# The up projection's 576 token columns cut at 384 in place of 288

## The chip, the cores and the metric

The kernel runs on one NeuronCore of one Trainium2 chip. The metric is device time in microseconds (us) of one execution; a lower number is better. Three timed runs of the kernel before took 1313.4, 1313.48 and 1315.09 us, a median of 1313.48 us. The profile is that of a further execution, whose span from the first to the last instruction was 1312.0 us. Instruction durations are in nanoseconds (ns).

## The reference, cut to what matters

The program is one layer of a hybrid decoder for 512 prompt tokens and 8 sequences of 8 sample tokens, 576 token columns in all. After a recurrent branch, an attention branch and their merge comes the part that the change touches, the gated feed-forward block with a short convolution over time:

```python
h2 = rmsnorm(x, norm2_g)
up, new_conv_f = causal_dwconv(jnp.einsum('btd,df->btf', h2, w_up), ffn_conv0, conv_f_w, conv_f_b)
gf, vf = jnp.split(up, 2, axis=-1)
x = x + jnp.einsum('btf,fd->btd', jax.nn.gelu(gf) * vf, w_down)
```

Here x has 1024 features, `w_up` is 1024 x 6144 and `w_down` 3072 x 1024, all float32. `causal_dwconv` adds three shifted copies of the rows, each scaled per feature, with two rows of state in front of every sequence.

## The kernel before, in words

Everything is kept with features on the 128 partitions and the 576 tokens along the free dimension: columns 0 to 511 are the prompt, 512 to 575 the eight samples.

A projection is made of **units**. One unit gives 128 output features for all 576 tokens and is accumulated in one of the two-bank PSUM tensors `ps[0]` and `ps[1]`, by turns (`ps[u % 2]`). Its first 288 token columns lie at element 0 (the first bank), the other 288 at element 512 (the second). `HALF` is 288. A unit of eight row tiles (k = 0 to 7) has 48 matmuls. To keep precision, weights and activations are each split into a rounded part and the rest (`w_hi`, `w_lo`, `h_hi`, `h_lo`, of type float32r), and three of the four products are added: `w_hi` by `x_hi`, `w_hi` by `x_lo`, `w_lo` by `x_hi`. Each product is two matmuls, one for each half of the tokens, with the same 128 x 128 weights. In the instruction stream each of these matmuls has a weight load (LDWEIGHTS) of its own ahead of it. All of this is `looped_unit` (L490 to L506), which `unit` (L486) calls, and which the other projections use too.

The feed-forward block has 24 **pairs** of up units, one for the gate features and one for the value features, so 48 up units, in three rounds, each followed by 8 down units. The order of work on TensorE is written out by hand: L833 to L835 are the first pair, `pairs` (L822) holds a loop over the other 8, 8 and 7 of a round, and `down` (L829) a down unit. A unit waits for its weights (`lo_ready`) and for its PSUM tensor to be free (`acc_free`).

Weights come by DMA on SyncE's queue, up to four units ahead (L348). ScalarE rounds them to `w_hi` (L862) and VectorE takes the difference to `w_lo` (L1168), each two units ahead of use.

When an up unit is done, VectorE runs `ffn_conv` (L1465): three multiplications by the reciprocal norm `rinv2` read the unit's columns from PSUM and put them in `ug` or `uv`: L1474 takes columns 0 to 287, L1475 columns 288 to 511, and L1476 the 64 sample columns, which go to a layout with room for the state rows. The third frees the PSUM tensor. Then come the difference of the next weights, three instructions of the convolution, and, after the pair's second unit, the product of gate and value (L1492 to L1505).

Of the kernel before, what the change touches and what calls it, by code (L numbers as in the profile page):

```python
# [7 lines left out]
ALU = mybir.AluOpType  # L8
# [6 lines left out]
KT = D // P  # L15
SEQ = 512
NB, NT = 8, 8
NS = NB * NT
TOK = SEQ + NS
HALF = TOK // 2  # L20
PAST = 256
NG, NH, HD = 3, 4, 128
AW = NG * NH * HD
# [25 lines left out]
UPAD, USEQ = 2, 2 + NT  # L49
US0 = UPAD + SEQ  # L50
UW = US0 + NB * USEQ
# [24 lines left out]
def up_unit(i):  # L76

    return U_FFN + 2 * i + KT * min((i - 1) // PPR if i else 0, NRND - 1)


def down_unit(r, m):
    pairs = min((r + 1) * PPR + 1, NPAIR)
    return U_FFN + 2 * pairs + KT * r + m
# [24 lines left out]
def build(nc, t):  # L108
# [33 lines left out]
    nkt = [u.shape[1] for u in units]  # L142

    ctx = ExitStack()
    with ctx:
        def sb(name, shape, dt=F32, at=ctx):
            return at.enter_context(nc.sbuf_tensor(name, shape, dt))
# [14 lines left out]
        h_hi = sb("h_hi", [P, KT, TOK], F32R)  # L162
        with ExitStack() as m:
            x_t = sb("x_t", [P, KT, TOK], at=m)
        h_lo = sb("h_lo", [P, KT, TOK], F32R)
# [74 lines left out]
        rinv2 = sb("rinv2", [P, TOK])  # L240
# [20 lines left out]
        ps = [ctx.enter_context(nc.psum_tensor(f"ps{i}", [P, 1024], F32)) for i in range(4)]  # L261
        acc = [p[:, :].rearrange("p (h n) -> p h n", h=2)[:, :, 0:HALF] for p in ps]
        NORM, TRN = 2, 3
# [37 lines left out]
        def diag(row):  # L301

            return row.rearrange("p (b n) -> p b n", n=NS + NT)[:, :, 0:NT]
# [32 lines left out]
        def seqs(ap, width):  # L336
            return ap.rearrange("p (b n) -> p b n", n=width)
# [145 lines left out]
        def _(pe):  # L483
            mm, tr = pe.matmul, pe.transpose

            def unit(u, x_hi, x_lo, ready=None, between={}):  # L486

                looped_unit(u % 2, nkt[u], u + 1, u // 2, x_hi, x_lo, ready, between)

            def looped_unit(p, n, parts, freed, x_hi, x_lo, ready=None, between={}):  # L490


                pe.wait_ge(lo_ready, parts)
                if not (isinstance(freed, int) and freed == 0):
                    pe.wait_ge(acc_free[p], freed)
                for k in range(n):
                    if k in between:
                        between[k]()
                    if ready:
                        ready(k)  # L500
                    for w, x in ((w_hi, x_hi), (w_hi, x_lo), (w_lo, x_hi)):
                        for h in range(2):
                            last = mm(ps[p][:, 512 * h:512 * h + HALF], w[:, p, k, :],  # L503
                                      x[:, k, HALF * h:HALF * (h + 1)],
                                      start=(k == 0 and x is x_hi and w is w_hi), stop=(k == n - 1 and w is w_lo))
                last.then_inc(unit_done, 1)  # L506

            def feature_sum(src, k, n):

                for h in range(2):  # L510
                    last = mm(ps[NORM][:, 512 * h:512 * h + HALF], ones, src[:, HALF * h:HALF * (h + 1)],  # L511
                              start=(k == 0), stop=(k == n - 1))
# [7 lines left out]
            for c in range(KT):  # L520
                last = tr(ps[NORM][:, c * NS:(c + 1) * NS], x_tok[0:NS, 4, c * P:(c + 1) * P], ident[0:NS, 0:NS])
# [240 lines left out]
            for c in range(KT):  # L762
                last = tr(ps[2][0:36, c * P:(c + 1) * P], l_st[:, c, :], ident)
            last.then_inc(lst_ps, 1)

            with pe.Fori(0, KT - 2) as i:
                for j, (tiles, hi, lo) in enumerate(((KT, h_hi, h_lo), (NH, att_hi, att_lo), (KT, h_hi, h_lo), (KT, y_hi, y_lo))):
                    u = U_MRG + 5 + j
                    looped_unit(u % 2, tiles, i * 4 + (u + 1), i * 2 + u // 2, hi, lo)
# [5 lines left out]
            def x2_products(c):  # L775

                if c < KT:
                    if c == 0:
                        pe.wait_ge(x2_in, 32)
                    else:  # L780
                        pe.wait_ge(x2_cp, c)
                    for n in range(4):
                        tr(ps[3][:, n * P:(n + 1) * P], x_tok2[:, n, c * P:(c + 1) * P], ident)
                    tr(ps[3][:, SEQ:TOK], x_tok2[0:NS, 4, c * P:(c + 1) * P], ident[0:NS, 0:NS]).then_inc(x2_ps, 1)
                if c:
                    pe.wait_ge(ones_rdy, 1)
                    pe.wait_ge(sq2_hi_rdy, c)
                    pe.wait_ge(sq2_lo_rdy, c)
                    for part in (sq2_hi, sq2_lo):
                        for h in range(2):  # L790
                            last = mm(ps[NORM][:, 512 * h:512 * h + HALF], ones_r[:, :],  # L791
                                      part[:, (c - 1) % 2, HALF * h:HALF * (h + 1)],
                                      start=(c == 1 and part is sq2_hi), stop=(c == KT and part is sq2_lo))
                    last.then_inc(sq2_used, 1)
# [27 lines left out]
            def pairs(first, count):  # L822

                with pe.Fori(0, count) as i:
                    for j in range(2):
                        u = up_unit(first) + j
                        looped_unit(u % 2, KT, i * 2 + (u + 1), i + u // 2, h_hi, h_lo)

            def down(r, m):  # L829
                unit(down_unit(r, m), g_hi[r % 2], g_lo[r % 2],  # L830
                     (lambda k: (pe.wait_ge(g_hi_rdy, r * PPR + k + 1), pe.wait_ge(g_lo_rdy, r * PPR + k + 1))) if m == 0 else None)

            unit(up_unit(0), h_hi, h_lo, lambda k: (pe.wait_ge(xg2_hi, k + 1), pe.wait_ge(xg2_lo, k + 1)),  # L833
                 {KT - 3: lambda: x2_products(KT)})
            unit(up_unit(0) + 1, h_hi, h_lo)  # L835
            for r in range(NRND):
                pairs(r * PPR + 1, min(PPR, NPAIR - 1 - r * PPR))
                down(r, 0)
# [1 line left out]
                if r < NRND - 1:  # L840
                    down(r, 1)
                    with pe.Fori(0, KT // 2 - 1) as i:
                        for j in range(2):
                            u = down_unit(r, 2) + j
# [316 lines left out]
        def _(dve):  # L1161
            STT, TT, TS = dve.scalar_tensor_tensor, dve.tensor_tensor, dve.tensor_scalar

            def lo_split(u):
                if u >= U_ALL:
                    return
                dve.wait_ge(hi_ready, u + 1)
                TT(w_lo[:, u % NSPL, 0:nkt[u], :], w_raw[:, u % NRAW, 0:nkt[u], :],  # L1168
                   w_hi[:, u % NSPL, 0:nkt[u], :], ALU.subtract).then_inc(lo_ready, 1)
# [128 lines left out]
            for hp in range(NH):  # L1298
# [18 lines left out]
                for g in range(NG):  # L1317
                    last = dve.tensor_copy(diag(q_dia[:, g, :]), qT[:, g, SEQ:TOK].rearrange("p (b t) -> p b t", b=NB))
                last.then_inc(q_dia_rdy, 1)
                for b in range(0, NB, 2):  # L1320
                    n = hp * NB + b
# [93 lines left out]
            for n, (kind, m) in enumerate(MERGE):  # L1415
                u = U_MRG + n
# [23 lines left out]
            for c in range(KT):  # L1440
                u = U_OUT + c
# [18 lines left out]
            def flinked(ins):  # L1460
                ins.then_inc(f_link, 1)
                flink[0] += 1
                dve.wait_ge(f_link, flink[0])

            def ffn_conv(i, j):  # L1465
                u, ti = up_unit(i) + j, i + j * FT
                x, y, v = (uv if j else ug)[:, i % 2, :], cv if j else cg, ft[:, ti, :]
                flinked(dve.tensor_copy(seqs(x[:, US0:UW], USEQ)[:, :, 0:UPAD], seqs(v[:, F_S:F_N], 2)))

                dve.wait_ge(unit_done, u + 1)  # L1470
                if i >= 2:
                    dve.wait_ge(fst_rdy, i - 1)
                p_ = ps[u % 2]
                TT(x[:, UPAD:UPAD + HALF], p_[:, 0:HALF], rinv2[:, 0:HALF], ALU.mult)  # L1474
                TT(x[:, UPAD + HALF:US0], p_[:, 512:512 + SEQ - HALF], rinv2[:, HALF:SEQ], ALU.mult)  # L1475
                TT(seqs(x[:, US0:UW], USEQ)[:, :, UPAD:USEQ], seqs(p_[:, 512 + SEQ - HALF:512 + HALF], NT),  # L1476
                   seqs(rinv2[:, SEQ:TOK], NT), ALU.mult).then_inc(acc_free[u % 2], 1)
                lo_split(u + NSPL)
                dve.wait_ge(acc_free[u % 2], u // 2 + 1)
                if j == 0 and i:  # L1480
                    dve.wait_ge(gm_rdy, i)
                flinked(TS(y[:, :], x[:, 0:CW], v[:, F_W:F_W + 1], v[:, F_B:F_B + 1], ALU.mult, ALU.add))
                flinked(STT(y[:, :], x[:, 1:1 + CW], v[:, F_W + 1:F_W + 2], y[:, :], ALU.mult, ALU.add))
                STT(y[:, :], x[:, 2:2 + CW], v[:, F_W + 2:F_W + 3], y[:, :], ALU.mult, ALU.add).then_inc(cv_rdy if j else cg_rdy, 1)
# [22 lines left out]
            for kind, i, m in ffn_steps():  # L1507
# [4 lines left out]
                else:  # L1512
                    u = down_unit(i, m)
# [6 lines left out]
def constants(np):  # L1520
# [13 lines left out]
    t = t[:, None]  # L1534
    k = np.arange(PAST)[None, :]
    own = [np.arange(P)[None, :] >= t,
# [34 lines left out]
```

## Time and profile before

| | |
|---|---|
| Median of the timed runs | 1313.48 us (1313.4 to 1315.09) |
| The profiled execution: span (the page gives no time beside it) | 1312.0 us |
| TensorE matmuls | busy 1269.2 us, 97% of the span, 9313 instructions |
| TensorE weight loads | busy 1223.8 us, 93%, 9313 instructions |
| VectorE | busy 727.9 us, 55% |
| ScalarE | busy 487.1 us, 37% |
| GpSimd | busy 167.0 us, 13% |

A matmul's record lasts from its start to the modelled end of its last column's way through the array, so records of matmuls that follow each other overlap. How fast they go is read from the distance between their starts, or from the time of a row that merges many, divided by their number. A row "x2" that starts at 786.07 and lasts 0.30 us, of instructions of 0.19 us each, has starts 0.30 - 0.19 = 0.11 us apart. The same goes for weight loads, which stand under PEld.

### The profile page before, as it was taken

What the parts mean: (1) busy time and instruction counts of PE and PEld (TensorE: products, weight loads), DVE (VectorE), ACT (ScalarE), POOL (GpSimd) and SP (SyncE); (2) the same over time, 40 slices, a digit from 0 to 9 for tenths busy, and PEclk for the clock granted to TensorE, in tenths of its full rate; (3) what the DMA queues carried; (4) which work ended last, traced back from release to release, by engine and by line L of the source; (5) the groups of instructions that cost most, each with busy time, mean ns of one, the idle gap of its engine ahead of it and who ended that gap; (6) DMA issues with size and microseconds to landing.
All of it is one profiled execution on the core that took longest, in us unless ns stands there. A gap on an engine that the chain in (4) does not pass through costs nothing.

```text
span 1312.0 us, 22213 instructions
## 1 busy us (share of the span) xinstructions
PE 1269.2 (97%) x9313; PEld 1223.8 (93%) x9313; DVE 727.9 (55%) x1212; ACT 487.1 (37%) x713; POOL 167.0 (13%) x255
## 2 busy tenths in 40 slices
PE   7899999999999999998999999999999999999996
PEld 6898998998899789998999999999999999999996
DVE  4973383283374348883333344788735886368821
ACT  4444444343443348774222234422222223122231
POOL 1271601601601100001000000000010001000021
PEclk9899999999999999999999999999999999999998
DMA  7382532522523112225323222232222223222321
GB/s 207 64 209 59 145 93 77 146 77 70 148 74 95 42 49 67 79 57 141 88 81 88 79 73 78 77 87 80 80 85 80 80 80 85 80 85 84 88 64 45
DMA packets 180436, 117.13 MB, mean 89 GB/s; under 512 B 6844, under 2 KB 172890, under 8 KB 180345
## 3 DMA queue, kind: packets, MB, share of 16 engines
q1 hardware_dynamic: 168944, 87.34, 23.5%
q0 software_dynamic: 11392, 28.79, 8.0%
q8 instruction: 49, 0.80, 0.3%
q14 instruction: 23, 0.19, 0.1%
q10 hardware_dynamic: 28, 0.01, 0.0%
HBM read 107.66 MB, written 8.45 MB: 89 GB/s over the span
## 4 chain that ended last, share of the span: by engine, by line
PE 92%; DVE 3%; ACT 2%; issue 1%; DMA 1%; POOL 0%; SPq 0%; ACTq 0%; POOLq 0%; DVEq 0%
PE ps L503 76%; PE ps L666 4%; PE ps L511 2%; PE ps L625 2%; PE ps L735 1%; PE ps L611 1%; PE ps L600 1%; DMA x_tok<-in_x_prompt 1%; PE ps L643 1%; PE ps L588 1%; DVE prob L1268 1%; DVE hn L1201 1%; ACT w_hi L862 0%; PE ps L791 0%; PE ps L808 0%
## 5 line engine op out<-in xcount | busy, mean ns | idle before, releaser
L503 PE MATMUL ps<-h_hi,w_hi 128*128 128x288 f32 x1824 | 404.0, 303 | 7.5 <-DVE h_lo L1204 3.9
L503 PE MATMUL ps<-h_hi,w_lo 128*128 128x288 f32 x1824 | 392.5, 297 | 0.0
L503 PE MATMUL ps<-h_lo,w_hi 128*128 128x288 f32 x1824 | 391.9, 297 | 0.0
L1168 DVE TENSOR_TENSOR w_lo<-w_raw,w_hi 128x1024 fp32r<-128x1024 f32 (+1 forms) x164 | 196.0, 1195 | 282.3 <-ACT w_hi L862 282.2
L862 ACT ACTIVATE w_hi<-w_raw 128x1024 fp32r<-128x1024 f32 (+1 forms) x164 | 170.3, 1038 | 445.3 <-PE ps L503 438.3
L503 PEld LDWEIGHTS ps<-h_hi,w_hi 128*128 128x128 f32 x1824 | 296.5, 190 | 12.4 <-issue 4.3
L503 PEld LDWEIGHTS ps<-h_lo,w_hi 128*128 128x128 f32 x1824 | 295.4, 190 | 0.0
L503 PEld LDWEIGHTS ps<-h_hi,w_lo 128*128 128x128 f32 x1824 | 295.3, 190 | 0.0
L1243 DVE RECIPROCAL qk_ri<-qk_rt 128x576 f32<-128x576 f32 x24 | 90.0, 3750 | 26.6 <-ACT qk_rt L941 26.6
L467 POOL DMA_DIRECT2D out<-f_row x12 | 6.2, 515 | 624.7 <-ACT f_row L1139 624.7
L503 PE MATMUL ps<-g_hi,w_hi 128*128 128x288 f32 x384 | 83.0, 297 | 1.6 <-DVE g_lo L1505 1.6
L503 PE MATMUL ps<-g_lo,w_hi 128*128 128x288 f32 x384 | 82.0, 295 | 0.0
L503 PE MATMUL ps<-g_hi,w_lo 128*128 128x288 f32 x384 | 82.0, 295 | 0.0
L503 PEld LDWEIGHTS ps<-g_hi,w_hi 128*128 128x128 f32 x384 | 61.5, 188 | 1.9 <-ACT g_hi L1132 1.8
L503 PEld LDWEIGHTS ps<-g_lo,w_hi 128*128 128x128 f32 x384 | 61.8, 188 | 0.0
L503 PEld LDWEIGHTS ps<-g_hi,w_lo 128*128 128x128 f32 x384 | 61.7, 188 | 0.0
L1132 ACT ACTIVATE g_hi<-gm 128x576 fp32r<-128x576 f32 x24 | 16.5, 686 | 91.8 <-DVE gm L1494 91.8
L625 PE MATMUL ps<-kcT,q_dia 128*64 128x128 f32 (+1 forms) x192 | 33.8, 315 | 1.4 <-DVE kcT L1325 1.4
L1325 DVE COPY kcT<-ps 128x512 f32<-128x512 f32 x16 | 11.1, 691 | 41.9 <-PE ps L611 41.9
L625 PEld LDWEIGHTS ps<-kcT,q_dia 128*64 128x64 f32 x192 | 22.0, 136 | 11.4 <-issue 4.0
L1268 DVE CUSTOM_DVE_ANT_0 prob<-ps,masks 128x512 f32<-128x512 f32 (+3 forms) x40 | 20.4, 546 | 18.9 <-PE ps L602 18.9
L1285 DVE TENSOR_SCALAR o_sb<-ps,stat 128x128 f32<-128x128 f32 (+1 forms) x20 | 7.0, 349 | 41.5 <-issue 32.0
(281 smaller groups left out, 1781.6 us busy)
## 6 DMA issues: line engine op xcount, KB each, us to landing
w_raw<-in_w_in SPq DMA_DIRECT2D x68, 512.0 KB, 3.9
w_raw<-in_w_up SPq DMA_DIRECT2D x48, 512.0 KB, 3.9
w_raw<-in_w_down SPq DMA_DIRECT2D x24, 512.0 KB, 3.9
vc<-in_cache_v_g POOLq DMA_DIRECT2D x12, 512.0 KB, 6.2
kc<-in_cache_k_g POOLq DMA_DIRECT2D x48, 128.0 KB, 3.1
w_raw<-in_w_br_a SPq DMA_DIRECT2D x8, 512.0 KB, 3.9
w_raw<-in_w_out SPq DMA_DIRECT2D x8, 512.0 KB, 3.9
x_tok<-in_x_prompt SPq DMA_DIRECT2D x4, 512.0 KB, 9.7
```

The lines of the kernel that those rows point to most:

```text
L503: last = mm(ps[p][:, 512 * h:512 * h + HALF], w[:, p, k, :], x[:, k, HALF * h:HALF * (h + 1)], start=(k == 0 and x is x_hi and w is w_hi), ...
L511: last = mm(ps[NORM][:, 512 * h:512 * h + HALF], ones, src[:, HALF * h:HALF * (h + 1)], start=(k == 0), stop=(k == n - 1))
L588: tr(bank[:, r * P:(r + 1) * P], src[:, r * P:(r + 1) * P], ident)
L600: mm(s[:, 0:SEQ], qT[:, 0, rows], kT[:, 0, 0:SEQ], start=True, stop=True)
L611: last = tr(bank[:, i * P:(i + 1) * P], kc[:, n % NKC, i, :], ident)
L625: last = mm(ps[2][0:NS, c0:c0 + cn], q_dia[:, g, (b - 1) * NS:b * NS], kcT[:, n % 2, c0:c0 + cn], start=(b == 1 and g == 0), stop=(b == NB ...
L666: last = mm(o_bank(hp, i), p_, v_, start=(n == 0), stop=(n == len(srcs) - 1))
L862: A(w_hi[:, u % NSPL, 0:nkt[u], :], w_raw[:, u % NRAW, 0:nkt[u], :], ACT.Copy).then_inc(hi_ready, 1)
L1132: A(g_hi[r % 2][:, i % PPR, :], gm[:, :], ACT.Copy).then_inc(g_hi_rdy, 1)
L1168: TT(w_lo[:, u % NSPL, 0:nkt[u], :], w_raw[:, u % NRAW, 0:nkt[u], :], w_hi[:, u % NSPL, 0:nkt[u], :], ALU.subtract).then_inc(lo_ready, 1)
L1243: dve.reciprocal(qk_ri[:, :], qk_rt[:, :]).then_inc(qk_rinv, 1)
L1268: last = dve.tensor_tensor_reduce(prob[0:rows, e % 2, s0:s0 + n], sc[0:rows, s0:s0 + n], masks[0:rows, m - C_PM:m - C_PM + n], SCALE, -3e3 ...
```

## The change

In the 48 up units, and only there, the first piece of the token columns becomes 384 wide (columns 0 to 383, at element 0 of the PSUM tensor) and the second 192 (columns 384 to 575, at element 512). `looped_unit` takes the width of the first piece as an argument, 288 unless told otherwise. The number of matmuls and weight loads, the total of the columns, the weights and the PSUM tensors are the same. In `ffn_conv` the reads follow: L1474 takes 384 columns, L1475 128, and L1476 the same 64 sample columns from their new place in the second bank.

```diff
+WIDE = 384
@@ looped_unit
-                        for h in range(2):
-                            last = mm(ps[p][:, 512 * h:512 * h + HALF], w[:, p, k, :],
-                                      x[:, k, HALF * h:HALF * (h + 1)],
+                        for at, c0, c1 in ((0, 0, first), (512, first, TOK)):
+                            last = mm(ps[p][:, at:at + c1 - c0], w[:, p, k, :], x[:, k, c0:c1],
                                       start=(k == 0 and x is x_hi and w is w_hi), stop=(k == n - 1 and w is w_lo))
@@ pairs, and the same at the two units of the first pair
-                        looped_unit(u % 2, KT, i * 2 + (u + 1), i + u // 2, h_hi, h_lo)
+                        looped_unit(u % 2, KT, i * 2 + (u + 1), i + u // 2, h_hi, h_lo, first=WIDE)
@@ ffn_conv
-                TT(x[:, UPAD:UPAD + HALF], p_[:, 0:HALF], rinv2[:, 0:HALF], ALU.mult)
-                TT(x[:, UPAD + HALF:US0], p_[:, 512:512 + SEQ - HALF], rinv2[:, HALF:SEQ], ALU.mult)
-                TT(seqs(x[:, US0:UW], USEQ)[:, :, UPAD:USEQ], seqs(p_[:, 512 + SEQ - HALF:512 + HALF], NT),
+                TT(x[:, UPAD:UPAD + WIDE], p_[:, 0:WIDE], rinv2[:, 0:WIDE], ALU.mult)
+                TT(x[:, UPAD + WIDE:US0], p_[:, 512:512 + SEQ - WIDE], rinv2[:, WIDE:SEQ], ALU.mult)
+                TT(seqs(x[:, US0:UW], USEQ)[:, :, UPAD:USEQ], seqs(p_[:, 512 + SEQ - WIDE:512 + TOK - WIDE], NT),
```

TensorE's order at the passage from the output projection (`mg_hi`, `mg_lo`: the merged branches) to the first up unit (`h_hi`, `h_lo`), before:

```order
L503 MATMUL ps<-mg_hi,w_hi 128x288 x2
L503 MATMUL ps<-mg_lo,w_hi 128x288 x2
L503 MATMUL ps<-mg_hi,w_lo 128x288 x2
L503 MATMUL ps<-h_hi,w_hi 128x288 x2
L503 MATMUL ps<-h_lo,w_hi 128x288 x2
L503 MATMUL ps<-h_hi,w_lo 128x288 x2
```

The same engine in the body of the loop over pairs, after the change, which has put the matmul on line 504:

```order
L504 MATMUL ps<-h_hi,w_hi 128x384
L504 MATMUL ps<-h_hi,w_hi 128x192
L504 MATMUL ps<-h_lo,w_hi 128x384
L504 MATMUL ps<-h_lo,w_hi 128x192
L504 MATMUL ps<-h_hi,w_lo 128x384
L504 MATMUL ps<-h_hi,w_lo 128x192
```

Nothing changes places; each couple of equal matmuls has become a wide one and a narrow one. VectorE's order at a gate unit, before and then after (`ft` holds the convolution's weights, `ps` the PSUM tensor):

```order
L1468 COPY ug<-ft 128x8x2
L1474 TENSOR_TENSOR ug<-ps,rinv 128x288
L1475 TENSOR_TENSOR ug<-ps,rinv 128x224
L1476 TENSOR_TENSOR ug<-ps,rinv 128x8x8
L1168 TENSOR_TENSOR w_lo<-w_raw,w_hi 128x1024
```

```order
L1468 COPY ug<-ft 128x8x2
L1474 TENSOR_TENSOR ug<-ps,rinv 128x384
L1475 TENSOR_TENSOR ug<-ps,rinv 128x128
L1476 TENSOR_TENSOR ug<-ps,rinv 128x8x8
L1168 TENSOR_TENSOR w_lo<-w_raw,w_hi 128x1024
```

Only the widths of the first two reads differ.

## Rows read from the trace of the kernel before

**Rows 1.** The profile page: span, engines, and granted clock in 40 slices

```profile
span 1312.0 us, 22213 instructions
PE 1269.2 (97%) x9313; PEld 1223.8 (93%) x9313; DVE 727.9 (55%) x1212; ACT 487.1 (37%) x713; POOL 167.0 (13%) x255
...
PEclk9899999999999999999999999999999999999998
```

**Rows 2.** Windows over the three rounds of up units: busy time of each engine

```profile
core 0: us, PE busy (x) PEld busy (x) DVE busy (x) ACT busy (x) POOL busy (x), PEclk, DMA share, GB/s
826.00:942.00 116.00, 116.00 (x872) 115.95 (x871) 95.86 (x200) 34.56 (x40) 0.00 (x0) 1.00 0.29 85
...
996.00:1098.00 102.00, 102.00 (x767) 102.00 (x766) 80.01 (x172) 25.90 (x30) 0.00 (x0) 1.00 0.29 82
...
1151.00:1240.00 89.00, 89.00 (x670) 89.00 (x669) 69.51 (x149) 22.41 (x26) 0.00 (x0) 1.00 0.29 83
```

**Rows 3.** Chain that ended last, from 826 us: start us, us, what, number

```profile
831.81 117.57 PE ps L503 x882
949.38 1.75 PE ps L808 x16
951.13 153.52 PE ps L503 x1152
1104.65 1.75 PE ps L808 x16
1106.39 134.03 PE ps L503 x1008
1240.50 1.07 ACT w_hi L862
```

**Rows 4.** Timeline of weight loads at 900 us, in an up unit

```profile
start us, us, engine line op out<-in xcount [idle before <-releaser]
...
900.02 0.32 PEld L503 LDWEIGHTS ps<-h_hi,w_lo 128*128 128x128 f32 x2
900.29 0.33 PEld L503 LDWEIGHTS ps<-h_hi,w_hi 128*128 128x128 f32 x2
```

**Rows 5.** Timeline of matmuls at 900 us, in an up unit

```profile
900.15 0.43 PE L503 MATMUL ps<-h_hi,w_lo 128*128 128x288 f32 x2
900.42 0.42 PE L503 MATMUL ps<-h_hi,w_hi 128*128 128x288 f32 x2
```

**Rows 6.** Groups of weight loads by form: busy us, mean ns of one

```profile
L503 PEld LDWEIGHTS ps<-h_hi,w_hi 128*128 128x128 f32 x1824 | 296.5, 190 | 12.4 <-issue 4.3 <-DVE w_lo L1168 3.3 <-ACT h_hi L895 1.3
...
L666 PEld LDWEIGHTS ps<-vc,p_dia 128*64 128x64 f32 x256 | 27.8, 137 | 0.5
L666 PEld LDWEIGHTS ps<-v_tok,probT 128*128 128x128 f32 x192 | 22.9, 192 | 0.0
```

**Rows 7.** Timeline of weight loads after an idle stretch at 785.9 us

```profile
785.86 0.14 PEld L784 LDWEIGHTS ps<-const,x_tok 64*128 64x128 f32 x1 [0.17 <-issue]
786.07 0.30 PEld L791 LDWEIGHTS ps<-sq_hi,ones_r 128*128 128x128 f32 x2
```

**Rows 8.** Timeline of weight loads at 133 us, in the attention

```profile
132.97 0.30 PEld L602 LDWEIGHTS ps<-kT,qT 128*128 128x128 f32 x2
133.19 0.75 PEld L666 LDWEIGHTS ps<-v_tok,probT 128*128 128x128 f32 x6
```

**Rows 9.** Timeline of matmuls at 132 us, in the attention

```profile
132.00 1.02 PE L600 MATMUL ps<-kT,qT 128*128 128x512 f32 x2
132.86 0.38 PE L601 MATMUL ps<-kT,qT 128*128 128x128 f32 x2
```

**Rows 10.** Timeline of matmuls at 18.7 us, plain float32 of 288 columns

```profile
18.75 1.14 PE L511 MATMUL ps<-sq,const 128*128 128x288 f32 x4
```

**Rows 11.** Groups of matmuls by form: busy us, mean ns of one

```profile
L511 PE MATMUL ps<-qk_sq,const 128*128 128x288 f32 x96 | 27.6, 411 | 0.0
```

**Rows 12.** Groups of VectorE by form, 826 to 942 us

```profile
L1474 DVE TENSOR_TENSOR ug<-ps,rinv 128x288 f32<-128x288 f32 x9 | 4.1, 458 | 0.3
...
L1475 DVE TENSOR_TENSOR ug<-ps,rinv 128x224 f32<-128x224 f32 x9 | 3.4, 380 | 0.0
```

More of the change, by code:

```diff
@@ L484, in _, with unit, looped_unit @@
             mm, tr = pe.matmul, pe.transpose
-            def unit(u, x_hi, x_lo, ready=None, between={}):
-                looped_unit(u % 2, nkt[u], u + 1, u // 2, x_hi, x_lo, ready, between)
-            def looped_unit(p, n, parts, freed, x_hi, x_lo, ready=None, between={}):
+            def unit(u, x_hi, x_lo, ready=None, between={}, first=HALF):
+                looped_unit(u % 2, nkt[u], u + 1, u // 2, x_hi, x_lo, ready, between, first)
+            def looped_unit(p, n, parts, freed, x_hi, x_lo, ready=None, between={}, first=HALF):
                 pe.wait_ge(lo_ready, parts)
@@ L833, in _ @@
             unit(up_unit(0), h_hi, h_lo, lambda k: (pe.wait_ge(xg2_hi, k + 1), pe.wait_ge(xg2_lo, k + 1)),
-                 {KT - 3: lambda: x2_products(KT)})
-            unit(up_unit(0) + 1, h_hi, h_lo)
+                 {KT - 3: lambda: x2_products(KT)}, first=WIDE)
+            unit(up_unit(0) + 1, h_hi, h_lo, first=WIDE)
             for r in range(NRND):
```

## The prediction, made before the changed kernel was run

> **What bounds the kernel now.** I read the page first: its engine rows show TensorE busy for 97% of the span, and the clock row full speed nearly throughout [rows 1]. The windows over the rounds of up units then show that nothing but TensorE counts there: it is busy for all of 116.00, 102.00 and 89.00 us, at a granted clock of 1.00 (the 2.4 GHz level), while VectorE has 95.86, 80.01 and 69.51 us and ScalarE less [rows 2]. The chain of waits says the same: three unbroken runs of L503 matmuls [rows 3]. So each nanosecond that an up unit gains or loses on TensorE is one of the total.
>
> Next, the pace inside such a run. 117.57 us for 882 matmuls is 133.3 ns from one to the next, 153.52 us for 1152 is 133.3, 134.03 us for 1008 is 133.0 [rows 3]. I take 133.3 ns, and 266.6 ns for a couple (the two pieces of one product). 288 columns at one per cycle of 2.4 GHz are 120.0 ns, so 13.3 ns of each interval is something else.
>
> Last, the weight loads, since each matmul has one. A load starts with the matmul ahead of it: loads at 900.02 and 900.29, matmuls at 900.15 and 900.42, each row a couple some 0.13 us apart, so that the second load of the row at 900.02 goes out with the matmul at 900.15 [rows 4, 5]. The load is hidden under a running matmul, and under one only. How long must that matmul be?
>
> - A load of 64 columns lasts 137 ns, one of 128 columns 192 [rows 6]: 55 ns for 64 columns, so 110 ns for the stream of 128 and the rest a fixed way through. The loads of L503 have the same form and 190 ns [rows 6].
> - After an idle stretch, when no earlier matmul holds anything up, two float32r loads start 0.30 - 0.19 = 0.11 us apart [rows 7]. The second can only be waiting for the first to have streamed.
> - Six loads in a row in the attention start (0.75 - 0.19) / 5 = 0.112 us apart [rows 8]. Their matmuls of 128 plain float32 columns stream at two cycles a column, 107 ns, so this is at or just above the load's own time.
>
> So a load needs about 110 ns. Under a matmul of 288 columns it fits. 192 columns stream in 192 / 2.4 = 80 ns, and it doesn't.
>
> The Trainium skill says of this, in "TensorE: Matmul & The Clock Gate", section "LDWEIGHTS (loading the stationary operand)", that a load takes its columns divided by 1.2 GHz, which is 107 ns here. [...]
>
> **The change part by part.** 48 up units of 8 row tiles of 3 products are 1152 couples, which now take 1152 x 266.6 ns = 307.1 us.
>
> *The wide piece*, 384 columns. No row shows a float32r matmul of another width than 288. If the 13.3 ns is a fixed cost, the interval is 160.0 + 13.3 = 173.3 ns. If it grows with the columns, it is 133.3 x 384 / 288 = 177.7. Plain float32 matmuls stream at two cycles a column. Two of 512 columns take from 132.00 to 132.86 us [rows 9], 430 ns each, where the columns need 427; four of 288 start (1.14 - 0.41) / 3 = 0.243 us apart, where the columns need 240 [rows 10, 11]. There the cost on top is 3 ns at both widths. That speaks for a fixed one, and gives the lower bound: if the long matmul sheds what it doesn't share with the plain ones, 160 + 3 = 163 ns. I take 174, nearest to the fixed cost.
>
> *The narrow piece*, 192 columns. Streaming alone gives 133.3 - 96 / 2.4 = 93.3 ns, the lower bound, if the next load were hidden all the same. With the load as the limit it is 108 to 112 ns by rows 7 and 8. Should the 288-column stream's surplus over a plain one, some 10 ns, come on top, 122, the upper bound. I take 113, which is row 8's value and a nanosecond for the turn.
>
> *The sum of a couple* is 174 + 113 = 287 ns, 20.4 ns more than now. 1152 x 20.4 ns = 23.5 us.
>
> *VectorE's reads.* 288 columns take 458 ns and 224 take 380 [rows 12]: 1.22 ns a column. 384 and 128 columns come to 575 + 263 = 838 ns, as now. They lie beside TensorE, which is the slower by 20 us in the first round [rows 2], and if that cover were gone the difference would still be nothing. No wait, DMA or buffer is added, and a unit's PSUM tensor is freed by the same third read, a whole unit of 6.4 us before TensorE wants it. The engines that wait for TensorE wait 24 x 20.4 ns = 0.49 us a unit longer and hold up nobody.
>
> The profiled execution has 1312.0 us from first to last instruction; the median of the runs is 1313.48, that is 1.5 us around the span. 1312.0 + 23.5 + 1.5 = 1337.0 us.
>
> **The rivals.**
>
> *A. The load limits the narrow matmul* (the forecast). For it: rows 6 to 8, three readings of 108 to 112 ns. Its own range: from 163 + 108 = 271 ns a couple (+4.4, times 1152 = 5.1 us, 1319 us) to 177.7 + 122 = 299.7 (+33.1, 38.1 us, 1352 us). Most of it lies above 1328, since the fixed cost is better borne out than its loss.
>
> *B. Not slower: loads are taken further ahead.* TensorE might start a second load while a wide matmul still runs, so that the load for the piece after the narrow one is partly done in the 174 ns of the wide one. Over a couple there are 266 ns of matmul for 220 ns of loading, so from full freedom in the order on, nothing would be lost: a couple stays at 266.6 ns and the kernel at 1313.5 us. It decides if a load can start before the matmul ahead of it does. Against it: in rows 4 and 5 each load waits for the start of a matmul, although it could have gone out 20 ns earlier. It might go so far as a gain, if besides the wide piece sheds its surplus: 163 + 93.3 = 256.3 ns, 1152 x 10.3 ns = 11.9 us less, 1302 us. The Trainium skill, in "TensorE: Matmul & The Clock Gate", section "Step-by-step: what each phase is for", lets TensorE pull loads ahead of running matmuls into a background set of weights. If that set is one deep, rows 4 and 5 agree with it and it gives no help here.
>
> *C. A narrow float32r matmul goes at the plain float32 rate.* A float32r column now costs one cycle. A plain product has two records (the two matmuls of a norm sum stand as x4), each at two cycles a column [rows 10]. If the one-cycle rate did not hold for short matmuls, 192 columns would take 2 x (160 + 3) = 326 ns, a couple 174 + 326 = 500 ns, and the kernel 1152 x 233.4 ns = 268.9 us more, 1582 us. No row speaks for it or against it, since all float32r matmuls here have 288 columns; that the same instruction is issued in both cases speaks against.
>
> *D. The change doesn't do what it says*: the pieces could come out as before. The order of instructions shows 384 and 192 in all up units, so I give this nothing.
>
> **How the numbers follow.** A has 0.79, B without a gain 0.10, B with a gain 0.04, C 0.07. The time predicted is A's, 1337.0 us. The range reaches from A's low end, 1319, to 1350, just under its high one, and holds nearly all of A. A change within 0.2% of 1313.5 us (2.6 us) is what a measurement can't tell from none. Faster by more than that is B with a gain, 0.04; the same is B without, 0.10; slower is A and C, 0.86.
>
> **What would show it.** In the profile after, matmuls of L504 with 192 columns should be followed by the next start after 110 to 115 ns, those with 384 after 173 to 178, and 48 matmuls of an up unit should take 6.9 us where 6.4 stood. The loads under a wide matmul should start with it, as now, and the load that goes out with a narrow one should be followed at once by its matmul, 110 ns later. TensorE stays 100% busy in the rounds at clock 1.00. The down units, still of 288 columns, should keep 133.3 ns. I am wrong if the next matmul starts 93 ns after a narrow one (B), or 300 ns and more (C), or if the whole time moves by something that isn't 1152 times the change of a couple.

## The result and the profile after

The changed kernel takes 1334.19 us, the median of three runs (1333.94 to 1336.15), against 1313.48 us: a ratio of 1.0159 with a 95% interval from 1.0142 to 1.0175. That is 20.7 us slower; 1337.0 was forecast, in a range from 1319 to 1350.

The page of the kernel after has the same number of instructions as [rows 1], and the growth of the span is all TensorE's:

```profile
span 1332.2 us, 22213 instructions
PE 1289.6 (97%) x9313; PEld 1244.4 (93%) x9313; DVE 728.8 (55%) x1212; ACT 487.0 (37%) x713; POOL 167.0 (13%) x255
```

TensorE is busy for 20.4 us more, the span is 20.2 us longer, the other engines do what they did. The windows over the first two rounds of up units, which stand beside [rows 2], show TensorE, and beside its weight loads nothing else, busy all the time, at the same clock (the 2.4 GHz level):

```profile
826.00:950.00 124.00, 124.00 (x875) 124.00 (x874) 96.17 (x200) 34.61 (x40) 0.00 (x0) 1.00 0.28 80
1004.00:1116.00 112.00, 112.00 (x792) 112.00 (x791) 83.38 (x178) 26.91 (x32) 0.00 (x0) 1.00 0.26 75
```

The chain of waits has the same pieces as [rows 3] (start us, us, what, number):

```profile
831.78 124.99 PE ps L504 x882
956.77 1.75 PE ps L808 x16
958.52 160.35 PE ps L504 x1152
1118.87 1.75 PE ps L808 x16
1120.62 139.99 PE ps L504 x1008
...
1270.59 6.40 PE ps L504 x48
```

The three long runs are 7.42, 6.83 and 5.96 us longer, 20.2 us together, which is the whole growth of the span. The last row is a down unit, still at 6.40 / 48 = 0.133 us a matmul. The first run holds one such unit and 834 matmuls of up units, so these take (124.99 - 6.40) / 834 = 142.2 ns each, and a couple of wide and narrow **284.4 ns**. The same sum on [rows 3] gives (117.57 - 6.40) / 834 = 133.3 and 266.6. The difference, 17.8 ns, times 1152 is 20.5 us. I use this sum below for each experiment, from its own first run.

Inside a couple, first the weight loads and then the matmuls of the kernel after, as in [rows 4, 5]:

```profile
899.88 0.19 PEld L504 LDWEIGHTS ps<-h_hi,w_hi 128*128 128x128 f32 x1
900.06 0.30 PEld L504 LDWEIGHTS ps<-h_lo,w_hi 128*128 128x128 f32 x2
900.35 0.30 PEld L504 LDWEIGHTS ps<-h_hi,w_lo 128*128 128x128 f32 x2
```

```profile
899.77 0.25 PE L504 MATMUL ps<-h_hi,w_lo 128*128 128x192 f32 x1
899.86 0.45 PE L504 MATMUL ps<-h_hi,w_hi 128*128 128x384 f32 x2
900.15 0.45 PE L504 MATMUL ps<-h_lo,w_hi 128*128 128x384 f32 x2
900.43 0.45 PE L504 MATMUL ps<-h_hi,w_lo 128*128 128x384 f32 x2
```

The load at 900.06 goes out with a narrow matmul. The second load of its row starts 0.30 - 0.19 = 0.11 us later, at 900.17. But the wide matmul started at 900.15: for the first time a load goes out behind its matmul and not with it. It had to wait for the load before it. That load is through by 900.28 (0.11 us on), and yet the next one, at 900.35, waits for the narrow matmul, which starts then. The wide matmul's record begins 0.09 us after the narrow one's (899.77, 899.86), before its weights are all in, and the next start comes 0.20 us later (900.06).

The trace keeps starts in whole nanoseconds, and I take their means over the up units from 845 to 935 us. The next matmul starts 87.2 ns after a narrow one and 197.3 ns after a wide one. The load that goes out with a narrow matmul is followed by the next after 108.2 ns, and that one by the next after 176.3 ns. Both pairs add up to the couple. The kernel with a short load, below, shows that a wide matmul without a wait takes 176 ns; so the wait of 108.2 - 87.2 = 21 ns is booked inside the wide matmul.

### The profile page after: what moved, and what is told of

It is laid out like the page before. It is cut to its first block, busy times and chain, and to the rows that moved or that the text cites. A ratio compares the mean times of both kernels' runs of the same rounds, so it can differ in the third digit from the quotient of the medians.

```text
span 1332.2 us, 22213 instructions
## 1 busy us (share of the span) xinstructions
PE 1289.6 (97%) x9313; PEld 1244.4 (93%) x9313; DVE 728.8 (55%) x1212; ACT 487.0 (37%) x713; POOL 167.0 (13%) x255
## 4 chain that ended last, share of the span: by engine, by line
PE 92%; DVE 3%; ACT 2%; issue 1%; DMA 1%; POOL 0%; SPq 0%; ACTq 0%; POOLq 0%; DVEq 0%
PE ps L504 76%; PE ps L666 4%; PE ps L511 2%; PE ps L625 2%; PE ps L735 1%; PE ps L611 1%; PE ps L600 1%; DMA x_tok<-in_x_prompt 1%; PE ps L643 1%; PE ps L588 1%; DVE prob L1268 1%; DVE hn L1201 1%; ACT w_hi L862 0%; PE ps L791 0%; PE ps L808 0%
## 5 line engine op out<-in xcount | busy, mean ns | idle before, releaser
L504 PE MATMUL ps<-h_hi,w_hi 128*128 128x288 f32 (+2 forms) x1824 | 412.1, 307 | 7.4 <-DVE h_lo L1204 3.9
L504 PE MATMUL ps<-h_hi,w_lo 128*128 128x288 f32 (+2 forms) x1824 | 400.7, 302 | 0.0
L504 PE MATMUL ps<-h_lo,w_hi 128*128 128x288 f32 (+2 forms) x1824 | 399.0, 300 | 0.0
L504 PEld LDWEIGHTS ps<-h_hi,w_hi 128*128 128x128 f32 x1824 | 288.3, 191 | 12.3 <-issue 4.2
L504 PEld LDWEIGHTS ps<-h_lo,w_hi 128*128 128x128 f32 x1824 | 286.8, 190 | 0.0
L504 PEld LDWEIGHTS ps<-h_hi,w_lo 128*128 128x128 f32 x1824 | 286.8, 190 | 0.0
L1243 DVE RECIPROCAL qk_ri<-qk_rt 128x576 f32<-128x576 f32 x24 | 90.0, 3751 | 26.6 <-ACT qk_rt L941 26.6
L1132 ACT ACTIVATE g_hi<-gm 128x576 fp32r<-128x576 f32 x24 | 16.4, 685 | 91.3 <-DVE gm L1494 91.3
L1474 DVE TENSOR_TENSOR uv<-ps,rinv 128x384 f32<-128x384 f32 x24 | 13.4, 558 | 49.8 <-issue 47.6
L1268 DVE CUSTOM_DVE_ANT_0 prob<-ps,masks 128x512 f32<-128x512 f32 (+3 forms) x40 | 20.4, 546 | 18.8 <-PE ps L602 18.8
```

The lines of the kernel that those rows point to most:

```text
L504: last = mm(ps[p][:, at:at + c1 - c0], w[:, p, k, :], x[:, k, c0:c1], start=(k == 0 and x is x_hi and w is w_hi), stop=(k == n - 1 and w i ...
L1132: A(g_hi[r % 2][:, i % PPR, :], gm[:, :], ACT.Copy).then_inc(g_hi_rdy, 1)
L1243: dve.reciprocal(qk_ri[:, :], qk_rt[:, :]).then_inc(qk_rinv, 1)
L1268: last = dve.tensor_tensor_reduce(prob[0:rows, e % 2, s0:s0 + n], sc[0:rows, s0:s0 + n], masks[0:rows, m - C_PM:m - C_PM + n], SCALE, -3e3 ...
L1474: TT(x[:, UPAD:UPAD + WIDE], p_[:, 0:WIDE], rinv2[:, 0:WIDE], ALU.mult)
```

## The experiments

**Other widths.** One constant is changed, on the changed kernel:

```diff
-WIDE = 384
+WIDE = 320        # and 352, and 448
```

320 and 256 columns:

> Pieces of 320 and 256 columns in the up units, nothing else. Three theories for the 17.9 ns that a couple of 384 and 192 lost (284.5 ns against 266.6 in the rounds of up units). Load: a weight load takes 111 ns and goes out no sooner than the narrow matmul, so a couple takes 111.2 + 13.3 + (columns of the wide piece) / 2.4 ns, or 266.6 if that is more. Here 257.8, so 266.6 stands: 1313.5 us, no change. Wide: a matmul above 288 columns pays by itself, 20.7 us for 96 columns more, so 6.9 us for 32: 1320.4. Short: every matmul under 256 columns pays a fixed surplus; here there is none: 1313.5.

352 and 224:

> Pieces of 352 and 224 columns. Load: 111.2 + 13.3 + 146.7 = 271.2 ns a couple, 4.6 over 266.6, times 1152 = 5.3 us: 1318.8 us. Wide: 64 / 96 of 20.7 = 13.8 us: 1327.3. Short: the full surplus, 20.7 us: 1334.2.

448 and 128:

> Pieces of 448 and 128 columns. Load: 111.2 + 13.3 + 186.7 = 311.2 ns a couple, 44.6 over 266.6, 51.4 us: 1364.9 us. Wide: 160 / 96 of 20.7 = 34.5 us: 1348. Short: 20.7 us as for 192: 1334.2.

The kernel before, run beside these, had a median of 1312.65 us. 320/256 took 1314.38 us, a ratio of 1.0013 (0.9998 to 1.0027); 352/224 took 1320.39, 1.0058 (1.0037 to 1.0078); 448/128 took 1367.19, 1.0412 (1.0385 to 1.044). The first run of the chain of each:

```profile
832.43 117.59 PE ps L504 x882
```

```profile
831.82 120.35 PE ps L504 x882
```

```profile
833.15 137.05 PE ps L504 x882
```

By the sum above that is 266.6, 273.3 and 313.3 ns a couple, where the load theory had 266.6, 271.2 and 311.2. The first is that of the kernel before to the nanosecond, although its wide piece has 32 columns more, so the wide theory falls. The theory of a fixed fine for short matmuls falls with the other two: 224 columns lose 6.7 ns, 192 lose 17.8, 128 lose 46.7. The loads of 448/128 show why it is that many:

```profile
900.25 0.30 PEld L504 LDWEIGHTS ps<-h_hi,w_lo 128*128 128x128 f32 x2
900.56 0.30 PEld L504 LDWEIGHTS ps<-h_hi,w_hi 128*128 128x128 f32 x2
```

Under a narrow matmul of 53 ns of columns the two loads are again 0.30 - 0.19 = 0.11 us apart. In the kernel of 352 and 224 columns, with 93 ns, they are too:

```profile
900.15 0.30 PEld L504 LDWEIGHTS ps<-h_hi,w_lo 128*128 128x128 f32 x2
```

The load does not shrink with the matmul above it: in the means over 845 to 935 us the two are 108.3, 108.2 and 108.3 ns apart under 224, 192 and 128 columns. The rest of the couple, from the second load to the next couple's first, is 165.0, 176.3 and 205.0 ns for the wide pieces of 352, 384 and 448. The load theory had 111.2 for the load, a number that was set to fit the changed kernel's couple, and 160.0, 173.3 and 200.0 for the rest. The first is too long by 3 ns and the rest too short by 3 to 5, which leaves 2.1 ns of error at 352 and at 448.

**The narrow piece first.** `WIDE = 192`:

> Pieces of 192 and then 384 columns: the narrow matmul comes first in each couple. Load: each narrow matmul still has one load under it and there are as many of them, so 20.7 us as with 384 and 192: 1334.2 us; in the records the interval after the narrow one is again some 87 ns and that after the wide one 197. If instead the order mattered (the last matmul of a product, which is followed by other weights, being the narrow one), most of the 20.7 us would go: near 1314.

1339.13 us, a ratio of 1.0206 (1.018 to 1.0232) to the same 1312.65 us, and 290.0 ns a couple, from this row:

```profile
831.92 127.32 PE ps L504 x882
```

The loss is there, as the load theory had it, and is not removed by the order. But it is 5.6 ns a couple larger than with 384 first, which no theory had. The loads are again 108 ns apart under the narrow piece (means as above); it is the other distance that has grown, from 176 to 182 ns.

**A shorter load.** In up units alone the weights get 64 columns, so half of the up projection's output features are left out, with pieces of 288 and 288, and of 384 and 192:

```diff
-                            last = mm(ps[p][:, at:at + c1 - c0], w[:, p, k, :], x[:, k, c0:c1],
+                            last = mm(ps[p][0:feat, at:at + c1 - c0], w[:, p, k, 0:feat], x[:, k, c0:c1],
```

288 and 288:

> Up units with weights of 64 columns in place of 128 (the other 64 output features of each up unit are not computed), pieces of 288 and 288 as before. A load then has half the stream, some 55 ns. Load theory: nothing was limited by loads at 288, so the couple stays near 266.6 ns and the time near 1313.5 us. If the 13.3 ns that a 288-column interval has over its columns came from the load running beside it, the couple would fall towards 246 ns and the kernel by up to 1152 x 20.6 ns = 24 us. This is the base for the next kernel.

384 and 192:

> The same 64-column weights (half of the output features of the up units left out) with pieces of 384 and 192. Load: a load of some 55 ns fits under the narrow matmul of 80 ns, so the couple costs what it costs with 288 and 288 and the same weights: no difference from the kernel beside it, and the interval records go to some 93 and 173 ns. Wide or short theory: the loss is in the matmuls themselves, and this kernel is 20.7 us slower than the one beside it.

The two took 1310.03 and 1311.13 us, beside 1313.37 us of the kernel before. Their first runs of the chain, in this order:

```profile
830.98 116.21 PE ps L505 x882
```

```profile
831.82 116.49 PE ps L505 x882
```

That is 263.3 and 264.0 ns a couple. With a load of half the stream, 384 and 192 cost 0.7 ns a couple more than 288 and 288, where they cost 17.8 with the full load. The loads go out with their matmuls again, in the second of the two kernels:

```profile
900.21 0.22 PEld L505 LDWEIGHTS ps<-h_hi,w_lo 128*64 128x64 f32 x2
900.47 0.22 PEld L505 LDWEIGHTS ps<-h_hi,w_hi 128*64 128x64 f32 x2
```

Its groups have 134 ns for one of them (busy us, mean ns, idle before):

```profile
L505 PEld LDWEIGHTS ps<-h_hi,w_lo 128*64 128x64 f32 x768 | 85.5, 134 | 15.8
```

So the two of a row start 0.22 - 0.134 = 0.086 us apart, which is the narrow matmul's own interval (in the means of the matmuls' starts 87.6 ns, and 176.4 for a wide one), and the load engine now sits idle between them. This is the experiment that settles the cause: the matmuls stream as many columns as in the changed kernel, and the load is half as long. Each matmul also gives 64 outputs in place of 128, which can't be told apart from the load by this pair alone; but both together are worth only 3.3 ns to the couple of 288 and 288, and 20.4 ns (284.4 - 264.0) to that of 384 and 192. The even couple has 26.6 ns over its columns, and 23.3 of them stay with the load halved, so most of that surplus has another cause.

**More couples.** The changed kernel with the down units cut in the same way. The diff shows those in the loop; the others get `first=WIDE` too, and VectorE adds each down unit in two instructions in place of one:

```diff
-                            looped_unit(u % 2, PPR, i * 2 + (u + 1), i + u // 2, g_hi[r % 2], g_lo[r % 2])
+                            looped_unit(u % 2, PPR, i * 2 + (u + 1), i + u // 2, g_hi[r % 2], g_lo[r % 2], first=WIDE)
```

> The changed kernel with the 24 down units cut at 384 and 192 as well (VectorE then adds a down unit in two instructions of 384 and 192 columns in place of one). 576 more couples. Load: each loses the same 17.9 ns, 10.3 us on top of 1334.2: 1344.5 us, and the down units before the last round of them run 48 matmuls in 6.83 us in place of 6.40. If the loss belonged to the up units alone (their loop, or VectorE's reads), nothing would be added: 1334.2 us.

1344.89 us, 10.7 us over the changed kernel (the kernel before, beside this one and the next two, took 1313.62), and a down unit takes

```profile
1285.95 6.81 PE ps L504 x48
```

in place of 6.40. 576 more couples cost what half of 1152 did. So the loss isn't a matter of the up units, their loop or VectorE's reads of them.

**Order or place.** The two other combinations of which piece comes first in time and which columns it has. Both have this edit, and the second has `WIDE = 192` besides:

```diff
-                        for at, c0, c1 in ((0, 0, first), (512, first, TOK)):
+                        for at, c0, c1 in (((0, 0, first), (512, first, TOK)) if first == HALF else ((512, first, TOK), (0, 0, first))):
```

The change's places, narrow issued first:

> The change's pieces at the change's places (columns 0 to 383 at element 0, 384 to 575 at element 512), but in each couple the narrow matmul is issued first. It asks why the kernel with 192 columns first took 290.0 ns a couple (87.5 and 202.5) in place of 284.5. If the order in time is the reason (the wide matmul last in its product), 290 ns and 1152 x 5.5 ns = 6.3 us over the changed kernel, about 1340 us. If it was where the wide piece lies (columns 192 to 575, second bank), the couple is back at 284.5 ns and the time at 1334 us. The load theory alone gives 284.5 ns for either.

Columns 192 to 575 issued first, then 0 to 191:

> Columns 0 to 191 at element 0, 192 to 575 at element 512, and the wide matmul issued first. The fourth of the four combinations of order and place. Order as the reason for the 5.5 ns: 284.5 ns a couple, 1334 us. Place as the reason: 290 ns, 1340 us.

1338.63 and 1334.18 us. The first runs of the chain:

```profile
829.23 127.32 PE ps L504 x882
```

```profile
831.97 124.99 PE ps L504 x882
```

290.0 and 284.4 ns a couple. The narrow piece in front costs 5.6 ns a couple wherever its columns lie, so it is the order and not the place. What in the order does it isn't shown. With the narrow piece first, the matmul behind the wide one belongs to the next product, so it has other weights or the other part of the activations (`h_lo` for `h_hi`); a kernel that issues the same product twice would tell more, and was not run.

## Why the prediction was right

The mechanism of forecast A is borne out, step by step. Two sizes were off, in opposite directions, and so was the place where the wait would be seen.

- *TensorE sets the end and each nanosecond counts*: the runs of the chain grew by 20.2 us, the span by 20.2.
- *A load needs about 110 ns and only one matmul hides it*: 108 ns between loads under pieces of 224, 192 and 128 columns, with 93, 80 and 53 ns of columns. With the load halved 0.7 of the 17.8 ns are left. Rival B (loads further ahead) is out: the late load goes out once the one before has streamed, and the load after it waits for the next matmul's start, although the load engine is free 0.07 us before that (900.28, 900.35).
- *The sum of a couple*: 287 ns were forecast and 284.4 measured, so 23.5 us became 20.5. The narrow term was put at 113 ns and is 108.2, by the distance of the loads. It came from the attention's loads, 0.112 us apart, and a nanosecond for a turn; but the matmuls beside those loads themselves need 107 ns and some 3 on top, so that row was an upper bound. The wide term was put at 174 ns, with the fixed 13.3 on top of its columns, and is 176.3. The two errors, 4.8 too much and 2.3 too little, partly cancel, and that much of the nearness of 287 is luck.
- *Where the wait would be seen*: this part was wrong. I expected the next start 110 to 115 ns after a narrow matmul and 173 to 178 after a wide one. The rows have 0.09 and 0.20 us. The wide matmul's record begins before its weights are in, and the wait is in it. By my own test ("I am wrong if the next matmul starts 93 ns after a narrow one") the reading would have gone to rival B, and only the couple's sum and the delayed load tell the two apart. The test should have been on the distance of the loads. The 48 matmuls of an up unit, forecast at 6.9 us, take 24 x 284.4 ns = 6.83.
- *VectorE's reads*, forecast as 575 and 263 ns for the same 838 as before. The groups after have 558 and 281, 839 together:

```profile
L1474 DVE TENSOR_TENSOR ug<-ps,rinv 128x384 f32<-128x384 f32 x24 | 13.4, 558 | 8.2 <-issue 7.5
...
L1475 DVE TENSOR_TENSOR ug<-ps,rinv 128x128 f32<-128x128 f32 x24 | 6.7, 281 | 0.0
```

  The PSUM tensor was said to be free a whole unit of 6.4 us before TensorE wants it. In the trace of the kernel before, the third read of a gate unit ends at 899.87 us and the tensor is wanted at 904.4, so it is some 4.5 us. That is still ample.

- *Rival C*, a narrow float32r matmul at a quarter of the rate, is out: 128 columns beside 448 take 313.3 ns, where C's way of counting gives 2 x (128 x 2 / 2.4 + 3) = 219 ns for the narrow piece and at least 448 / 2.4 = 187 for the wide one, 406 together; and 0.7 ns is all that 192 columns lose once the load is short.
- *On top of the sum*: 1.5 us between span and median were assumed; it was 1334.19 - 1332.2 = 2.0.

## What to carry to other kernels

Where TensorE sets the time and every matmul reloads its weights, as here, each piece of moving columns has to be long enough to cover the next load by itself; what a longer neighbour has to spare helps nothing. The even cut is safe as long as its half covers a load; here 256 columns lose nothing and 224 already lose 6.7 ns a couple. Read that limit from the distance of two loads that nothing else holds up, and judge the result by the sum over a couple, not by the start of the next matmul.

## What the runs showed of the hardware

The time that a float32r matmul takes on top of its columns grows with their number here. With the load out of the way (64-column weights, 384 and 192), the next start comes 87.6 ns after the narrow matmul and 176.4 after the wide one: 7.6 and 16.4 ns over the columns, or 0.456 and 0.459 ns a column, where a cycle at the granted clock is 0.417. I had taken the 13.3 ns for a fixed cost, since plain float32 matmuls have 3 ns at either width [rows 9 to 11]. Pieces of 288 and 288 and of 320 and 256 come to the same 266.6 ns, which fits both readings, but the starts inside the second couple don't: 149.3 ns after 320 columns and 117.3 after 256 are 16.0 and 10.6 over. The growth isn't a clean one; 352 columns have 18.3 over (165.0 - 146.7), 384 have 16.3 and 448 again 18.3. What slows the stream wasn't looked for.

The second surprise is the 5.6 ns of the order, above.
